# Output projection inside the head loop, modulation units 26 and 27 beside the queries, dense residual ahead of late column sums, transposes between the router's halves

## The reference, cut to what matters

```python
def modulate(x, g, shift, scale):
    return rms_norm(x, g) * (1 + scale[:, None, :]) + shift[:, None, :]
...
for l in range(DEPTH):
    mod = c_act @ ada_w[l] + ada_b[l]
    sh1, sc1, g1, sh2, sc2, g2 = jnp.split(mod, 6, axis=-1)
    ...
    x = x + (1 + g1[:, None, :]) * y
    h = modulate(x, ffn_norm[l], sh2, sc2)
    ...
    x = x + (1 + g2[:, None, :]) * y
```

## Time and profile before

| | us |
|---|---|
| median of three runs | 1435.01 |
| profiled execution, device time | 1435.28 |
| its span | 1433.3 |
| TensorE busy | 1393.2 (97%) |
| VectorE busy | 417.0 (29%) |
| ScalarE busy | 292.8 (20%) |
| first expert matmul, from the span's start | 512.00 |

### The profile page before, as it was taken

The page is one execution under the profiler, slowest core; times in us unless marked ns, Lnnn a source line. Parts: engine busy times, 40 slices in busy tenths (PEclk is TensorE's granted clock), DMA queues, the critical chain, the costliest instruction groups (busy, mean ns, idle before and its releaser), DMA issues.

```text
span 1433.3 us, 33502 instructions
## 1 busy us (share of the span) xinstructions
PE 1393.2 (97%) x15573; PEld 1044.5 (73%) x15574; DVE 417.0 (29%) x759; ACT 292.8 (20%) x519; POOL 30.4 (2%) x50
## 2 busy tenths in 40 slices
PE   7999999999988999999999999999999999999997
PEld 3887999999446876667767766776776776776774
DVE  2795998987667410000000000000000000000000
ACT  3562444443445210110010010000000000001001
POOL 1000000000000020000000000000000000000000
PEclk9999999999999999999999999999999999999999
DMA  9999588999640569999999999999999999999990
GB/s 353 345 380 338 175 291 314 317 324 328 237 186 4 232 229 371 373 392 369 402 408 382 401 408 384 402 408 386 397 407 396 390 403 398 392 402 399 398 383 15
DMA packets 172830, 484.39 MB, mean 338 GB/s; under 512 B 6416, under 2 KB 33264, under 8 KB 172688
## 3 DMA queue, kind: packets, MB, share of 16 engines
q1 hardware_dynamic: 170288, 474.17, 87.2%
q0 software_dynamic: 1680, 5.90, 1.7%
q10 hardware_dynamic: 720, 2.14, 0.4%
HBM read 476.95 MB, written 5.24 MB: 336 GB/s over the span
## 4 chain that ended last, share of the span: by engine, by line
PE 92%; SPq 3%; DVE 2%; ACT 1%; issue 1%; DMA 0%; POOL 0%; ACTq 0%; DVEq 0%
PE psum L1944 36%; PE psum L1947 26%; PE psum L1722 5%; PE psum L1723 5%; PE psum L1724 5%; PE psum L1638 3%; PE psum L1516 3%; SPq L585 2%; PE psum L1790 2%; PE psum L1609 2%; PE psum L1676 2%; PE psum L1771 1%; PE psum L1560 1%; PE psum L1590 0%; DMA ring<-in_a_gx_w 0%
## 5 line engine op out<-in xcount | busy, mean ns | idle before, releaser
L1947 PE MATMUL psum<-ring,xe 128*32 128x256 f32 x2688 | 591.4, 379 | 0.0
L1944 PE MATMUL psum<-ring,xe 128*32 128x512 f32 (+1 forms) x5376 | 590.0, 486 | 0.7 <-ACT xe L929 0.7
L1947 PEld LDWEIGHTS psum<-ring,xe 128*32 128x32 f32 x2688 | 292.9, 110 | 96.3
L1944 PEld LDWEIGHTS psum<-ring,xe 128*32 128x32 f32 x5376 | 219.9, 110 | 83.2 <-issue 5.2
L1947 PE MATMUL psum<-ring,hT 128*32 128x256 f32 x1152 | 254.4, 379 | 0.0
L1944 PE MATMUL psum<-ring,hT 128*32 128x512 f32 (+1 forms) x2304 | 253.9, 486 | 0.0
L1429 DVE TENSOR_TENSOR hs<-sg,psum 128x768 f32<-128x768 f32 x24 | 22.9, 954 | 643.8 <-PE psum L1947 643.8
L1947 PEld LDWEIGHTS psum<-ring,hT 128*32 128x32 f32 x1152 | 125.9, 110 | 40.6
L1722 PE MATMUL psum<-fh,dhi 128*128 128x256 f32 x384 | 109.9, 286 | 3.7 <-DVE fl L1243 2.5
L1944 PEld LDWEIGHTS psum<-ring,hT 128*32 128x32 f32 x2304 | 93.8, 110 | 24.5
L966 ACT ACTIVATE hT<-psum 128x768 f32<-128x768 f32 x24 | 19.5, 811 | 445.3 <-PE psum L1516 445.3
(11 more groups left out here) (277 smaller groups left out, 1280.5 us busy)
## 6 DMA issues: line engine op xcount, KB each, us to landing
ring<-in_m_w_gu SPq DMA_DIRECT2D x96, 2048.0 KB, 13.4
ring<-in_m_w_down SPq DMA_DIRECT2D x56, 2048.0 KB, 13.0
ring<-in_ada_w SPq DMA_DIRECT2D x24, 2048.0 KB, 15.7
ring<-in_m_w_gu SPq DMA_DIRECT2D x32, 1024.0 KB, 11.2
ring<-in_f_w_gu SPq DMA_DIRECT2D x24, 1024.0 KB, 14.2
ring<-in_f_w_down SPq DMA_DIRECT2D x6, 2048.0 KB, 14.8
ring<-in_a_w_in SPq DMA_DIRECT2D x4, 2048.0 KB, 19.4
ring<-in_kv_ada_w SPq DMA_DIRECT2D x4, 2048.0 KB, 8.3
```

The source lines that it names most:

```text
L1944: mm(banks[TB * j:TB * j + TB, c0:c0 + n], block(j, j), w[:, c0:c0 + n], start=first, stop=last, skip_group_check=True)
L1947: ins = mm(banks[TB * TBLKS:, 256 * r:256 * r + 256], block(TBLKS, r), w[:, 768:1024], start=first and r % 2 == 0, stop=last, skip_group_c ...
```

## The change

Four things.

1. The residual of the dense layer no longer waits for the sums of units 23 and 24 (now the list `ADA_LATE`). Their sums, copies and turns follow `stats(2)` and ScalarE's Sqrt; the keep-clocks around are 10 and 12 where 8 and 16 stood.
2. VectorE's chunks of units 26 and 27 stand behind `qk(2)` and `qk(3)`, with `H` as their accumulator; the column sums go to a corner of bank 3 and stand on TensorE directly behind the loop.
3. The output projection is turned around: `o_products(k, blocks)` multiplies chunk `k` of `A` into blocks, with all eight blocks open in banks 0, 1, 7 and 2. Inside the loop, turns 2 to 7 issue six blocks of chunk p - 2 where two keep-clocks stood. The other two blocks of chunks 0 to 5, and all blocks of chunks 6 and 7, follow the loop. The residual waits for `o_full` pair by pair, all statistics follow, then 17 keep-clocks.
4. Eight of the 16 row transposes stand between the router's chunks 3 and 4, the others behind it; ScalarE copies the four banks in the order 0, 2, 1, 3.

The pieces below follow the order: tables, ScalarE, VectorE, TensorE.

```diff
-        ada_acc = lambda v: (sqb if v % 4 < 2 else qw)[:, v % 2, :]
+        ada_acc = lambda v: (H[:, 2 * (v - 26):2 * (v - 26) + 2, :].rearrange("p k n -> p (k n)") if v >= 26 else
+                             (sqb if v % 4 < 2 else qw)[:, v % 2, :])
...
+        ADA_LATE = [v for v in range(10, 10 + ADA_IN_DENSE) if ada_turn_at_step.get(v, DSTEPS) >= DSTEPS]
...
-            unit(("o", i), cols_of(b_w_o[0], i * UC), task_end(7 + 2 * i))
+            unit(("o", i), cols_of(b_w_o[0], i * UC), (o_full, 2 * i + 2))
...
+        ada_bank = lambda v: bank[2 + v % 2] if v < 26 else bank[3][:, 4 * (v - 26):4 * (v - 26) + 4]
...
+        o_half = lambda a: bank[(0, 1, 7, 2)[a // 2]][:, SEQ * (a % 2):SEQ * (a % 2) + SEQ]
...
                 then(nc.scalar.activation(rms[:, :], stat_bank(q)[:, 0:SEQ], ACT.Sqrt, bias=eps[:, 0:1]), rmss)
+                if q == 2:
+                    for v in ADA_LATE:
+                        ada_copy(v)
...
+            act.wait_ge(ada_mm, 28)
             norm(3, [(H, 32, 88)], KC // 2)
...
-            for i in range(4):
-                act.wait_ge(ht_tp, i + 1)
+            for at, i in enumerate((0, 2, 1, 3)):
+                act.wait_ge(ht_tp, at + 1)
+                if i >= 2:
+                    act.wait_ge(h_more, KC // 2)
...
+            def residual_o():
+
+                for k in range(KC):
+                    dve.wait_ge(o_full, k // 2 + 1)
+                    then(v_.scalar_tensor_tensor(out=xT[:, k, :], in0=o_half(k), scalar=gate1[:, 16 + k:17 + k],
+                                                 in1=xT[:, k, :], op0=ALU.mult, op1=ALU.add), xs if k % 2 else None)
...
             norm(2)
+            for v in ADA_LATE:
+                ada(v)
...
                 qk(T)
                 if T == 1:
                     ada(25)
+                if T == 2:
+                    dve.wait_ge(acc_full[1], 1)
+                    ada_chunks(26)
+                elif T == 3:
+                    ada_chunks(27)
...
-            residual(6, 2, lambda i: ada_chunks(26 + i) if i < 2 else None)
+            residual_o()
...
-            for v in ada_summed_by(PAIRS_DENSE):
+            keep_clock(bank[0][:, :], 10)
+
+            stats(2)
+            for v in ADA_LATE:
                 ada_sums(v)
                 ada_turn(v)
-            keep_clock(bank[0][:, :], 8)
-
-            stats(2)
-            keep_clock(bank[0][:, :], 16)
+            keep_clock(bank[0][:, :], 12)
...
+            def o_products(k, blocks):
+
+                pe.wait_ge(o_evac, k + 1)
+                for a in blocks:
+                    w = columns(("o", a // 4))
+                    last = mm(o_half(a), w[:, k, (a % 4) * P:(a % 4 + 1) * P], A[:, k, :],
+                              start=k == 0 and a % 2 == 0, stop=k == KC - 1, skip_group_check=True)
+                    if k == KC - 1 and a % 2:
+                        last.then_inc(o_full, 1)
...
-                keep_clock(bank[0][:, :], 2)
+                if p == 2:
+                    wait_free(pe, 5)
+                    pe.wait_ge(qkT_done, 6)
+                if p < 2:
+                    keep_clock(bank[0][:, :], 2)
+                else:
+                    o_products(p - 2, range(6))
                 probs_T(p)
             values(NH // 2 - 1)
-            pe.wait_ge(o_evac, KC)
-            for i in range(2):
-                project(("o", i), A, after_tile=lambda tk, i=i: stats(3, [2 * i + tk - 1]) if i or tk else None)
-            stats(3, [3])
+            pe.wait_ge(sc_evac, NH // 2)
             for v in (26, 27):
                 ada(v)
-            keep_clock(bank[0][:, :], 7)
+            for k in range(6):
+                o_products(k, (6, 7))
+            o_products(6, range(8))
+            o_products(7, range(8))
+            stats(3)
+            keep_clock(bank[0][:, :], 17)
...
+                if k == KC // 2 - 1:
+                    h_rows_of(0)
+                    h_rows_of(2)
             last.then_inc(rt_mm, 1)
...
+            h_rows_of(1)
+            h_rows_of(3)
```

More of the change, by code:

```diff
@@ L269, in build @@
         o_evac = sem("o_evac")
+        o_full = sem("o_full")
         rt_mm = sem("rt_mm")
@@ L501, in build @@
             job_at.append(per_job[i % RING])
-        acc_tasks = 10
+        acc_tasks = 6
         ACC_FREE_AT = {T: T // 2 + 1 for T in range(6)}
@@ L836, in _ @@
             for v in range(10, 10 + ADA_IN_DENSE):
-                if ada_sum_at_step.get(v, DSTEPS) + WB >= DSTEPS:
+                if v not in ADA_LATE and ada_sum_at_step[v] + WB >= DSTEPS:
                     ada_copy(v)
@@ L1191, in _ @@
                 then(v_.tensor_tensor(C[:, k, :], C[:, k, :], B[:, k, :], ALU.mult), mxd)
[L1193 to L1204, removed]
-                            then(ins, xs)
+            def residual_o():
[3 more added lines that the diff above has]
+                                                 in1=xT[:, k, :], op0=ALU.mult, op1=ALU.add), xs if k % 2 else None)
             def dense_lo(n):
@@ L1264, in _ @@
             for v in range(10, 10 + ADA_IN_DENSE):
-                if ada_turn_at_step.get(v, DSTEPS) + WB + 1 >= DSTEPS:
+                if v not in ADA_LATE and ada_turn_at_step[v] + WB + 1 >= DSTEPS:
                     ada(v)
@@ L1375, in _ @@
                                       ALU.mult, ALU.add), hm)
+            dve.wait_ge(ada_mm, 28)
             for v in (26, 27):
@@ L1580, in ada @@
                 for i in range(UC // P):
-                    last = mm(bank[2 + v % 2][:, i:i + 1], ada_acc(v)[:, i * P:(i + 1) * P], ones[:, 0:1],
+                    last = mm(ada_bank(v)[:, i:i + 1], ada_acc(v)[:, i * P:(i + 1) * P], ones[:, 0:1],
                               start=True, stop=True)
@@ L1597, in ada_turn @@
                 transposed(bank[2 + v % 2][:, P:2 * P], sums[:, :], ident[:, :]).then_inc(ada_mm, 1)
-            def project(name, src, after_tile):
-                w = columns(name)
-                for tk in range(2):
-                    T, b = acc_bank()
-                    for a in range(2):
-                        i = 2 * tk + a
-                        for k in range(KC):
-                            last = mm(b[:, SEQ * a:SEQ * a + SEQ], w[:, k, i * P:(i + 1) * P], src[:, k, :],
-                                      start=k == 0, stop=k == KC - 1)
-                    last.then_inc(acc_full[T % 2], 1)
-                    after_tile(tk)
             stats(0)
@@ L1877, in _ @@
                               start=k == 0 and n == 0, stop=k == KC - 1, skip_group_check=True)
+                if k == KC // 2 - 1:
+                    h_rows_of(0)
+                    h_rows_of(2)
             last.then_inc(rt_mm, 1)
-            for T in (acc_tasks - 2, acc_tasks - 1):
-                wait_free(pe, T)
-            for i in range(4):
-                for a in range(4):
-                    last = transposed(rows_bank(i)[:, a * P:(a + 1) * P],
-                                      H[:, 4 * (i % 2) + a, (i // 2) * P:(i // 2 + 1) * P], ident[:, :])
-                last.then_inc(ht_tp, 1)
+            h_rows_of(1)
+            h_rows_of(3)
             pe.wait_ge(mask_ready, 1)
```

18 lines of the change are left out of this document (9 added, 9 removed).

## The result

Measured: 1439.63 us (median of 10 runs, 1437.80 to 1443.24) against 1434.74 for the kernel before on the same chip (10 runs, 1433.28 to 1440.04); ratio **1.0026**, 95% interval 1.0014 to 1.0037. The ratios in this document are estimates over all runs of both kernels, not quotients of the printed medians; those give 1.0034 here, and 0.9980 in experiment 5 where the ratio is 0.9967, so a difference of 0.001 between two ratios decides nothing. The forecast was 1433.5 with a range to 1436.2: wrong in sign and outside the range. The profiled execution took 1438.95 us, its span 1437.0, 3.7 more than before; the mean granted clock of TensorE is 0.989 against 0.993.

What follows compares the result with a forecast made beforehand. It took the expert stage as 921.3 us of TensorE-bound matmuls that the change can only start earlier; -1.6 + 3.5 + 12.1 - 15.9 + 0.4 = -1.5 us gave 1433.5 against the median, range 1429.6 to 1436.2.

Steps and rivals of the forecast that it cites:

- Step 1: End of dense layer: residual ahead of the late sums lets the K/V product start earlier, -1.6 us.
- Step 2: Queries: units 26 and 27 on VectorE there are not fully covered by its waits, +3.5 us.
- Step 3: Head loop: output products lengthen a turn from 3.29 to 5.45 us, +12.1 us over six turns.
- Step 4: Behind the head loop, values 7 to Sqrt: 18.6 us instead of 34.5, -15.9 us.
- rival C: Clock falls before the fifth router chunk, 1435.9; with a second half-clock stretch in the loop's products, 1437.8; chance 0.13.
- Step 5: Router, Sqrt to first expert matmul: with transposes between its halves and the clock falling again, 21.8 us against 21.4, +0.4.
- D: Queries: units 26 and 27 are covered by VectorE's waits after all, so their 3.5 us vanish, 1430.0; chance 0.08.
- B: Router: the clock stays at 2.4 GHz because transposes break the router up, 1430.4; chance 0.27.

Runs made afterwards that it cites:

- experiment 5: Changed kernel with VectorE's chunks of units 26 and 27 in the head loop's waits and their column sums behind the statistics: 1432.49 us, ratio 0.9967 to the kernel before.
- experiment 7: Kernel before with only the dense residual put ahead of the two late sums, keep-clocks 10 and 12: 1434.35 us, ratio 0.9995.
- experiment 1: Changed kernel with the column sums of units 26 and 27 back behind the last statistics: 1436.00 us, ratio 1.0003 to the kernel before.
- 14: Changed kernel with the router in one piece and the column sums of units 26 and 27 behind the statistics: 1434.45 us, ratio 0.9987 to the kernel before.
- 15: Changed kernel with the router in one piece, column sums behind the statistics, units 26 and 27 in the head loop: 1430.10 us, ratio 0.9945 to the kernel before.
- experiment 3: Changed kernel with keep-clocks in two TensorE waits for VectorE, 10 before the fourth transposes, 12 before the last query's: 1437.93 us, ratio 1.0013 to the kernel before.
- experiment 9: As experiment 6, but the router in one piece with all sixteen transposes behind it: 1426.72 us, ratio 0.9930 to the kernel before.
- experiment 6: As experiment 5, plus ten keep-clocks ahead of the last query's transposes: 1430.95 us, ratio 0.9967 to the kernel before.

## Why the prediction was wrong, by its steps

**Step 1 held** in mechanism and size: residual at 360.83 (361.5 less 0.76 is 360.74), K/V product at 371.63 (371.5). At the median its 1.6 us don't stand out from nothing (experiment 7).

**Step 2 held in the trace**: scores at 415.08 against 414.9. VectorE's fourth block ends at 409.04 and TensorE's transposes wait 2.67 us for it. Moving the units into the loop took 3.9 and 3.7 us off S (experiments 1 to 5 and 14 to 15), near the forecast's 3.5. In the ratios it gave more, 0.36% with step 5 in and 0.42% without, 5 to 6 us, but both are uncertain by about 0.2%, so 3.5 us is not excluded. That the half clock behind this wait is a part of the price is argued, not shown: in the profiled execution it slowed six query passes from 2.74 to 3.93 us, but VectorE was then the later of the two. The Trainium skill (TensorE: Matmul & The Clock Gate, "HAM oscillation") says that a wait, there one for a transfer, between bursts of matmuls lets the next burst start at half clock. The trace agrees in this place (a wait for VectorE, 0.66 of full clock in 408 to 413); behind the 3.09 us of idle at 430.94 the transposes ran at full clock and the fall came 2 us later.

**Step 3's turn held**: 5.54 us against 5.45. The first turn took 443.68 - 436.86 = 6.8 us, since the half-clock stretch ran on to 439.7 where it had ended at 433.0. That is the first step that failed, "so I let the cost stand as it is": +1.4 us for the first turn (5.54 in experiment 3, at full clock), +0.4 for five turns of 5.54, and 0.2 that values 1 came late: 471.36 for values 7 against 469.4.

**Step 4 was right at full clock and wrong in the run.** Values 7 to Sqrt took 22.2 us against 18.6: column sums 2.2 instead of 1.7, products 474.65 to 489.77, 15.1 instead of 12.2, because the clock was at 0.50 for 7 us of them; the rest in the statistics. This is the mechanism of rival C's second part, a half-clock stretch in the products, which I had priced at 3.5 us long, 1437.8, and given a part of C's 0.13. It was 7 us long. With full clock (experiment 3) the sum of steps 1 to 4 comes out at 120.96 against 121.05. That match is closer than its parts: up to values 1 it is 0.9 short (the forecast had kept the half clock of 430 to 433, which is absent there; that it is the whole of the 0.9 isn't shown), the six turns are 0.5 over and the part behind values 7 0.3 over. So no term of work was off by more than 0.5 us; what was missing is a term for the clock. Taking the column sums off the path gave 0.0023 with step 5 in and 0.0010 without, 1.4 to 3.3 us, of which the forecast had 1.7.

**Step 5 is the step furthest off at the median:** some 3.4 us (0.0024) against +0.4. It isn't alone in the sign, since experiment 1 came to 1.0003 with step 5 in. Its number in the trace looks right, 22.08 against 21.8. But its reasoning fell: "Eight transposes between the halves of the router partly fill a wait for VectorE's half of H: router end 8.9" behind the Sqrt. There is no wait to fill. In the changed kernel VectorE's half of H starts at 498.88, its first chunk there 0.44 us later, and the router's first half ends at 499.8. So the transposes go on the path in full, 0.9 us at full clock and 1.75 at half, and the mask starts that much later; the router ended 10 us behind the Sqrt. Before, all sixteen lay beside the mask and overran it by 0.3 us. And I compared with one execution, X 21.41, in which the clock had fallen inside the router. Without step 5 X was 18.26, 20.08, 20.12, 21.41, 21.60 and 23.04 in six profiles; with it, never under 22.08 in eleven; the means are 20.8 and 22.8. The lower half of that spread, not 21.41, was the thing to lose.

**The other rivals.** D fell: the units were not covered beside the queries, they are in the loop. B (the clock stays up because transposes break the router) fell in all eleven profiles. The rule that I had weighed (the Trainium skill, the same page, "Part 4: PE-mode transpose": full clock doesn't engage for transposes) pointed the right way: in experiment 9 the clock fell a third into sixteen transposes in a row, behind a router at full clock. But the row shows the router's 8-column passes and the transposes in one sequence and can't say which of them let it fall. Transposes do run at full clock while it lasts: eight in 1.07 us at 499.80 in the changed kernel.

**The clock over all runs** bears the missing term out beyond the single profiles. The mean granted clock is 0.9908 over the 109 runs of the kernel before in the experiments, and 0.9881 over the changed kernel's ten. A straight line through those 109 runs gives 0.87 us for each 0.001 of clock, so an estimated 2.4 us of the loss go with the clock, or 0.0027 x 1437 = 3.9 if TensorE's work filled all of the half-clock time. Undoing step 5 went with a higher mean clock each time (though on another chip): 0.9881 to 0.9900 in the changed kernel, 0.9893 to 0.9902, 0.9902 to 0.9917 and 0.9918 to 0.9945 in the next three columns of the table; step 5 alone, on one chip, had 0.9897 against 0.9912. That is 0.0017 in the mean, by the same two estimates 1.5 to 2.4 us of step 5's 3.4; the transposes on the path are 0.9 at full clock.

The trace of the changed kernel adds up: 5.7 late at the Sqrt (2.0 of it at values 7, 3.6 behind), 0.3 behind it, less the 0.76 that this execution was early: 5.2 over the forecast's 1431.8 of span, 1437.0. At the median the parts weigh differently (over forecast: step 5 about 3, column sums 0 to 1.6, units 2, the last two within the noise). They overlap and each has an uncertainty of some 2 us, so their sum is no account to the microsecond.

**The version to keep** is experiment 9: dense residual ahead, output products in the head loop, units 26 and 27 in the loop's VectorE waits, column sums behind the statistics, ten keep-clocks in the last query's wait, the router in one piece. It beats the kernel before by 0.7% on one chip, and the changed one, measured on another chip against the same kernel, by 0.9930 / 1.0026, about 1.0%.

## What to carry to other kernels

Before a gap is filled, find its row (idle before, and who ended it): the gap in the router wasn't there, the ones in the long TensorE-bound loop were, and those beside the queries belonged to a phase that alternates between two engines. A new wait on TensorE, or small matmuls before a long stretch, are priced with that stretch at half clock too. A distance from one profile with a half-clock stretch in it is no baseline: look in several runs how short it gets.

## What the runs showed of the hardware

The granted clock varies between executions of the same kernel, and the time with it: of 35 runs of the kernel before, the 8 with a mean clock of 0.993 took 1434.4 us in the mean and the 8 with 0.988 took 1439.8. That spread of 5.4 us is as large as what was being measured, so a single profile tells which stretches can fall and not how often they do.

The clock can fall inside a stretch in which TensorE shows no idle time at all. 49 us into the expert stage stand 32 matmuls of two columns. In ten of the seventeen profiles of this study a stretch at half clock follows or overlaps them, and there the expert stage is 922.7 to 924.4 us long; in the seven without it 921.2 to 921.7. Experiment 5 (first the small matmuls on TensorE, then busy time by stage):

```profile
557.37 3.18 PE L1956 MATMUL psum<-tg,pick 128*96 128x2 f32 x32
```

```profile
560.00:563.00 3.00, 3.00 (x22) 1.61 (x25) 0.32 (x2) 0.00 (x0) 0.00 (x0) 0.50 1.03 414
```

and the changed kernel, where the same matmuls stand at 564.54:

```profile
564.54 2.88 PE L1953 MATMUL psum<-tg,pick 128*96 128x2 f32 x32
```

```profile
568.00:572.00 4.00, 4.00 (x59) 2.42 (x55) 0.00 (x0) 0.00 (x0) 0.00 (x0) 1.00 1.03 410
```

It costs 1.5 us where it happens once; in experiment 6, where the stretch was 6.8 us long, 3.1. What decides it was not tried.
